# Base products in one fp32r pass, the bias's low part moved to VectorE, embedding norm on VectorE with its constants on ScalarE's queue

## The chip, the core and the metric

The kernel runs on one core of a Trainium2 chip. The engines are PE (TensorE), DVE (VectorE), ACT (ScalarE), POOL (GpSimd) and SP (SyncE, which only issues transfers); each works through its own instruction list in order and waits on semaphores. The metric is the device time of one execution in microseconds. TensorE's clock has two levels here, 1.2 and 2.4 GHz; the profile gives the granted clock as a share of the full one.

## What is computed

The reference chains two transformer blocks over 512 tokens of width 1024. Only the first is touched:

```python
h = _layernorm(jnp.concatenate([meta, x], axis=1), ln_emb_g, ln_emb_b)      # 16 + 512 rows
mix = _mixer(h, ...)                                                         # MLA and GQA attention
h = _layernorm(DEEPNORM_ALPHA * h + mix, ln1_g[i], ln1_b[i])
logits = h @ w_router + b_router;  top_val, top_idx = top_k(logits, 4);  gates = softmax(top_val)
hgu = ragged_dot(h[tok], w_gate_up, group_sizes) + b_gate_up[e_sorted]       # 32 experts
out = ragged_dot(_clamped_swiglu(hgu), w_down, group_sizes) + b_down[e_sorted]
h = _layernorm(DEEPNORM_ALPHA * h + segment_sum(out * gate), ln2_g[i], ln2_b[i])
```

All arithmetic is fp32. Large products are made of fp32r parts: each operand is split into a high part (rounded to fp32r) and a low part (the rest), and the product is high x high + high x low + low x high, each a single-pass matmul. A plain fp32 product is the two-pass matmul that the trace shows as two records.

## The kernel before

Tokens lie in NT = 4 tiles of 128 rows, plus a fifth tile of the 16 meta rows. Every engine's list is written out by hand; `past(name, n)` waits for the n-th signal of that name, `signal` and `put` give one. Buffers are slices of two large SBUF tensors, `act` and `ring`; a name such as `act_parts` in the profile is the same memory seen as fp32r.

**Start.** SP issues the four x tiles, the meta rows, then `colc` (constants in columns, with the epsilon that ACT's square root needs), `lnG`, `lnB` (gain and shift, broadcast to 128 rows), `cm` (the matrices that PE's transposes need) and the weights `w_in` (L1059 to L1071). On DVE, `stats` (L1575, L1578) of tile t runs ahead of `normalise` (L1580 to L1590) of tile t-1: reciprocal, subtract and scale, times gain. POOL's `shift` (L2191 to L2198) adds `lnB`. PE turns each tile (L373), ACT and DVE copy the halves out (L1213, L1622), and block 1's first products follow. The other norms use `affine` on DVE: two `scalar_tensor_tensor` with a reciprocal between them (L1592 to L1606).

**Routing.** After the mixer's output products, `routed_tile` picks four experts a token; then DVE computes gates, ranks and the lists (L1797 to L1900). PE multiplies the one-hot tiles of each token tile into `list_psum`, and DVE takes from it the token list `tl_i`, the places `to_i` and `slot_gate`. POOL then copies a column of the list and gathers 128 rows of `h1_d` (L2277, L2280). Item i of the expert loop is 128 such rows of one expert. Behind the lists DVE splits chunks 4 and 5 of expert 0 (`chunk_low`, L1743); 0 to 3 were split earlier, between the tiles of norm 1.

The bias of gate_up is applied as a 64-row product: `bias2` holds its high part in rows 0 to 31, its low part in rows 32 to 63, and `sel` picks the expert. SP loads `b_gate_up` twice (L1126, L1127) after six chunks of expert 0 and after the last tile of norm 1. POOL adds 1 to the up half (L2264), ACT rounds (L1341), and POOL subtracts to get the low part (L2266). PE waits for `bias_lo` before turning the first rows.

**Item 0.** `turn_rows` (L644), ACT's high part (L1349), DVE's low part `rows_low` (L1912), then `gate_up(0)`: the first half (hh = 0, chunks 0 to 3), `base()`, the second half. `base()` makes the gate-weighted sum of `b_down` for all 512 tokens: 8 products (4 tiles, 2 halves) of `GT` (gates turned to 32 rows by L635, copied by ACT L1343) with `bd` (32 rows) in fp32. DVE adds each to the residual (`base`, L1919), then POOL writes the running sums `acc_d` (L2322, L2323):

```python
for n in range(2 * NT):
    t, hf = n // 2, n % 2
    if n >= 4:
        eng.wait_ge(*past("based", n - 3))
    mm(PS[:, 4 + n % 4, :], GT[:, t, :], bd[:, hf * 512:(hf + 1) * 512]).then_inc(...)
```

SP loads chunks 10 and 11 of expert 0 and chunks 4 to 7 of expert 1 only after the sums' transfers (`sums_begun`, L1130 on).

**Loop.** Each pass loads 12 chunks of 1 MB, ACT rounds them (L1314), DVE makes the low parts (L1743), PE computes gate_up of item i and down of item i-1. PSUM has eight banks: gate_up uses 0 to 3, down 4 and 5, turned rows 6 and 7.

## Time and profile before

| | us |
|---|---|
| median of 3 runs | 2459.7 (2457.81 to 2460.18) |
| the profiled execution | 2455.43, span 2453.6 |
| PE busy | 2321.6 (95%) |
| DVE busy | 1674.0 (68%) |
| ACT busy | 1206.9 (49%) |
| POOL busy | 369.6 (15%) |
| mean DMA rate over the span | 226 GB/s |

"Busy" sums the instructions of an engine; a line can be that of a helper (L365 is `mm`, L373 `turn`'s transpose), so one line holds many products. A bracket behind a row of the timeline says how long the engine had been idle before it and what released it. The windows give, for each stretch, the busy time of each engine (with its count of instructions), the granted clock and the share and rate of the DMA engines.

### The profile page before, as it was taken

How to read it: one execution, taken by the hardware profiler on the slowest of the kernel's cores; microseconds unless marked ns; L12 is line 12 of the kernel's file. 1: busy time of each engine (PE TensorE's matmuls, PEld its weight loads, DVE VectorE, ACT ScalarE, POOL GpSimd, SP SyncE). 2: the span in 40 equal slices, each digit the busy share in tenths (PEclk: the TensorE clock that was granted, in tenths of full speed). 3: DMA queues.
4: the chain of work that ended last, by engine and by line, in shares of the span. 5: the costliest groups of instructions: out<-in, count | busy, mean ns of one | idle time of the engine just before them, and what ended most of it. 6: DMA issues, size and time to landing. Idle time of an engine off the chain costs nothing.

```text
span 2453.6 us, 29282 instructions
## 1 busy us (share of the span) xinstructions
PE 2321.6 (95%) x10464; PEld 1831.5 (75%) x10464; DVE 1674.0 (68%) x1669; ACT 1206.9 (49%) x1189; POOL 369.6 (15%) x267
## 2 busy tenths in 40 slices
PE   5989886999999999999999999959999999999998
PEld 3649654788888888888888888848676787888887
DVE  4535565889889889889988988953555636532434
ACT  1123421767767767776776776723333532331320
POOL 2033002112212212221221221210120001000000
PEclk9999986999999999999999999979999999999999
DMA  8010134999999999999999999772210132322220
GB/s 295 1 52 22 59 143 150 343 384 368 368 392 367 367 388 372 368 383 376 367 378 381 368 374 385 255 265 82 86 48 35 69 122 101 120 77 96 103 103 35
DMA packets 142131, 555.00 MB, mean 226 GB/s; under 512 B 11392, under 2 KB 12416, under 8 KB 125104
## 3 DMA queue, kind: packets, MB, share of 16 engines
q1 hardware_dynamic: 129248, 509.77, 54.6%
q0 software_dynamic: 11088, 40.11, 6.3%
q10 hardware_dynamic: 1728, 4.20, 0.4%
q8 instruction: 45, 0.74, 0.1%
q14 instruction: 22, 0.18, 0.0%
HBM read 525.73 MB, written 28.31 MB: 226 GB/s over the span
## 4 chain that ended last, share of the span: by engine, by line
PE 78%; DVE 3%; ACT 1%; DMA 1%; issue 1%; POOL 0%; DVEq 0%; ACTq 0%; POOLq 0%
PE PS L365 75%; PE PS L650 1%; PE PS L644 1%; ACT ring_parts L1417 0%; DVE ring_parts L1981 0%; DVE act L1601 0%; PE PS L840 0%; DVE st L1575 0%; DVE act L1606 0%; PE PS L750 0%; DMA act<-c_bias_ext 0%; DMA acc_d<-act,to_c 0%; DMA act<-h_d,tl_c 0%; ACT act L1488 0%; DVE act L2178 0%
## 5 line engine op out<-in xcount | busy, mean ns | idle before, releaser
L365 PE MATMUL PS<-act_parts 128*128 128x512 f32 (+2 forms) x3316 | 1064.9, 398 | 23.0 <-DVE act_parts L1891 13.2
L1743 DVE TENSOR_TENSOR low<-ring,act_parts 128x2048 fp32r<-128x2048 f32 x396 | 886.5, 2292 | 45.3 <-ACT act_parts L1314 45.2
L365 PEld LDWEIGHTS PS<-act_parts 128*128 128x128 f32 (+1 forms) x3316 | 622.4, 190 | 189.0 <-issue 58.4
L1314 ACT ACTIVATE act_parts<-ring 128x2048 fp32r<-128x2048 f32 x396 | 732.2, 1911 | 19.1 <-PE PS L365 18.8
L365 PE MATMUL PS<-low,act_parts 128*128 128x512 f32 x1584 | 620.3, 392 | 0.0
L365 PE MATMUL PS<-act_parts,ring_parts 128*128 128x512 f32 (+1 forms) x1280 | 380.1, 388 | 0.6 <-DVE act_parts L2112 0.6
L365 PEld LDWEIGHTS PS<-low,act_parts 128*128 128x128 f32 x1584 | 299.7, 189 | 58.4
L365 PEld LDWEIGHTS PS<-act_parts,ring_parts 128*128 128x128 f32 x1280 | 239.7, 191 | 59.6 <-issue 12.0
L1981 DVE TENSOR_TENSOR ring_parts<-ring,ring_parts 128x4096 fp32r<-128x4096 f32 x30 | 132.7, 4423 | 211.4 <-ACT ring_parts L1417 211.4
L365 PE MATMUL PS<-ring_parts,act_parts 128*128 128x512 f32 x1088 | 262.8, 394 | 2.1 <-DVE act_parts L2144 2.1
L365 PEld LDWEIGHTS PS<-ring_parts,act_parts 128*128 128x128 f32 x1088 | 204.9, 189 | 48.2 <-issue 4.8
L365 PE MATMUL PS<-ring_parts 128*128 128x512 f32 (+1 forms) x608 | 232.3, 382 | 0.0
L365 PE MATMUL PS<-act 128*128 128x128 f32 (+8 forms) x960 | 176.1, 340 | 12.9 <-POOL act L2227 9.6
L1417 ACT ACTIVATE ring_parts<-ring 128x4096 fp32r<-128x4096 f32 x30 | 108.7, 3624 | 136.3 <-PE PS L365 127.9
L365 PEld LDWEIGHTS PS<-act 128*128 128x128 f32 (+2 forms) x960 | 129.7, 196 | 32.9 <-issue 21.4
L1359 ACT ACTIVATE act<-PS 128x512 f32<-128x512 f32 x66 | 39.4, 597 | 206.0 <-PE PS L365 206.0
L365 PEld LDWEIGHTS PS<-ring_parts 128*128 128x128 f32 x608 | 116.2, 191 | 22.2 <-issue 1.5
L2301 POOL DMA_INDIRECT acc_d<-act,to_c x33 | 111.2, 3371 | 27.1 <-POOL to_c L2298 27.1
L1364 ACT ACTIVATE act_parts<-PS 128x512 fp32r<-128x512 f32 x66 | 39.0, 591 | 135.0 <-PE PS L650 135.0
L2287 POOL CAST act_parts<-act 64x128 fp32r (+1 forms) x34 | 59.4, 1748 | 259.2 <-PE PS L365 259.2
L2298 POOL COPY to_c<-to_i 128x1 int32 x33 | 35.2, 1067 | 409.7 <-ACT act L1370 409.7
L365 PE MATMUL PS<-act,ring 128*128 128x512 f32 (+3 forms) x272 | 91.4, 494 | 0.4 <-issue 0.4
(230 smaller groups left out, 1727.5 us busy)
## 6 DMA issues: line engine op xcount, KB each, us to landing
ring<-w_gate_up SPq DMA_DIRECT2D x264, 1024.0 KB, 8.1
ring<-w_down SPq DMA_DIRECT2D x132, 1024.0 KB, 7.5
ring<-w_ff SPq DMA_DIRECT2D x16, 2048.0 KB, 7.7
ring<-w_in SPq DMA_DIRECT2D x12, 2048.0 KB, 9.1
ring<-w_o SPq DMA_DIRECT2D x1, 4096.0 KB, 22.8
ring<-w_out SPq DMA_DIRECT2D x2, 2048.0 KB, 8.4
acc_d<-ring POOLq DMA_DIRECT2D x5, 512.0 KB, 3.1
act<-x SPq DMA_DIRECT2D x4, 512.0 KB, 4.9
```

The source lines that it names most:

```text
L365: return eng.matmul(o, lhsT, rhs, start=first, stop=last, **kw)
L644: ins = eng.transpose(PS[:, 6 + k // 4, k % 4 * P:(k % 4 + 1) * P], xg.rearrange("s (p k) -> s k p", k=KD)[:, k, :], ident)
L650: ins = eng.transpose(PS[:, 6 + hh, j * P:(j + 1) * P], gb[:, hh, :].rearrange("s (m j) -> s j m", j=4)[:, j, :], ident)
L1314: A_(W1hi[c % CS], W1[c], ACT.Copy).then_inc(sem["high"], 1)
L1359: A_(sg[:, hh, :].rearrange("s (b m) -> s b m", b=2), gate_up[:, :, :, 0], ACT.Sigmoid, scale=1.702).then_inc(sem[f"sig_done{hh}"], 1)
L1364: A_(aThi[:, hh, :], PS[:, 6 + hh, :], ACT.Copy).then_inc(sem[f"aT_high{hh}"], 1)
L1417: A_(W2hi[n % NH], W2[n % NW], ACT.Copy).then_inc(signal("w_high"), 1)
L1743: tt(W1lo[c], W1[c], W1hi[c % CS].bitcast(F32), ALU.subtract).then_inc(sem["low"], 1)
L1981: tt(W2lo[n % NW], W2[n % NW], W2hi[n % NH].bitcast(F32), ALU.subtract).then_inc(signal("w_low"), 1)
L2287: eng.tensor_copy(sel, selall[:, bass.ds(n, 1)].to_broadcast([2 * E, P])).then_inc(sem["sel_ready"], 1)
L2298: eng.tensor_copy(to_c[:, :], to_i[:, bass.ds(i - 2, 1)]).then_inc(sem["places_named"], 1)
L2301: eng.indirect_dma_start(out=acc_d, out_offset=bass.IndirectOffsetOnAxis(ap=to_c[:, 0:1], axis=0), in_=yb, in_offset=None, compute_op=ALU. ...
```

## The change

Three parts.

1. Base products: `Gf3` holds, for each tile, the gates' high part, low part and high part again (96 columns); PE turns them to 96 rows `GT`, and `bd3` holds `b_down`'s high part twice and its low part (`bd` is loaded three times; ACT rounds it after `list_psum`, DVE subtracts in rows 64 to 95). One fp32r matmul over 96 rows makes each product. Products 0 to 3 stand ahead of `gate_up`'s first half and use banks 4, 5, 2, 3; products 4 to 7 stand between the halves and use 4 to 7. The second half waits for the first four sums. On DVE the first four sums stand ahead of `chunk_low` of chunks 4 to 7; chunks 4 and 5 are no longer split behind the lists.
2. Bias: SP loads `b_gate_up` after the second tile of norm 1 and ahead of the six chunks; the low part is made by DVE behind the lists. PE waits for `bias_lo` in `gate_up`.
3. Embedding norm: `affine` on DVE in place of `normalise` and POOL's `shift`; `affine` takes 16 rows for the meta tile. ACT issues `colc`, `lnG`, `lnB` and `cm` as its first instructions.

The diff, with most of the unchanged lines left out:

```diff
@@ -85,7 +85,7 @@
...
     "ln_std": [("ln0_std", 5)] + [(f"ln{n}_std", 4) for n in range(1, 5)],
-    "ln_scaled": [("ln0_scaled", 5)],
+    "ln_scaled": [],
     "ln_out": [("ln0_out", 5)] + [(f"ln{n}_out", 4) for n in (1, 2, 3)] + [("ln4_out", 8)],
@@ -219,7 +219,7 @@
...
         Mm = v(R0 + 1248, NT, E)
-        Gf = v(5744, NT, E)
+        Gf = v(R0, NT, E)
         ge = v(R0 + 1504, NT, E)
@@ -242,9 +242,11 @@
...
         OHL = [part(3072, TOPK, 3 * (ITEMS + 1)), part(5120, TOPK, 3 * (ITEMS + 1))]
-        GT = v(5120, NT, P, parts=E)
+        GT = part(5120, NT, P, parts=3 * E)
+        Gf3 = part(5744, NT, 3 * E)
+        bd3 = part(3072, D, parts=3 * E)
         pad = v(5696, ITEMS + 1)
-        bd = v(4096, D, parts=E)
+        bd = v(4096, D, parts=3 * E)
         wr = v(11488, KD, E)
@@ -559,7 +561,7 @@
...
             def router(t):
-                eng.wait_ge(*past("router_in", 48))
+                eng.wait_ge(*past("router_in", 80))
                 eng.wait_ge(*past("h1T_act", t + 1))
@@ -627,12 +629,12 @@
...
 
-            eng.wait_ge(*past("gated", 1))
+            eng.wait_ge(*past("gates_split", 3))
             b = next_bank()
...
             for t in range(NT):
-                ins = eng.transpose(PS[0:E, b, t * P:(t + 1) * P], Gf[:, t, :], ident)
+                ins = eng.transpose(PS[0:3 * E, b, t * P:(t + 1) * P], Gf3[:, t, :].bitcast(F32), ident)
             ins.then_inc(put("gT_psum", b), 1)
@@ -652,7 +654,6 @@
...
             eng.sem_inc(sem["down_used"], 4)
-            eng.wait_ge(*past("bias_lo", 1))
             eng.wait_ge(sem["rows_in"], 16)
@@ -667,18 +668,27 @@
...
 
-            def base():
-                for n in range(2 * NT):
-                    t, hf = n // 2, n % 2
-                    if n >= 4:
-                        eng.wait_ge(*past("based", n - 3))
-                    mm(PS[:, 4 + n % 4, :], GT[:, t, :], bd[:, hf * 512:(hf + 1) * 512]).then_inc(
-                        put("base_psum", 4 + n % 4), 1)
+            def base(n):
+                t, hf = n // 2, n % 2
+                if n == 0:
+                    eng.wait_ge(*past("gT_out", 1))
+                    eng.wait_ge(*past("bd_low", 1))
+                if n >= 4:
+                    eng.wait_ge(*past("based", n - 3))
+                b = (4, 5, 2, 3, 4, 5, 6, 7)[n]
+                mm(PS[:, b, :], GT[:, t, :], bd3[:, hf * 512:(hf + 1) * 512]).then_inc(put("base_psum", b), 1)
 
             def gate_up(i, again=True):
+                if not again:
+                    for n in range(4):
+                        base(n)
                 eng.wait_ge(sem["xT_low"], i + 1)
                 eng.wait_ge(sem["sel_ready"], i + 1)
+                if not again:
+                    eng.wait_ge(*past("bias_lo", 1))
                 for hh in range(2):
+                    if not again and hh:
+                        eng.wait_ge(*past("based", 4))
                     if again:
@@ -692,7 +702,8 @@
...
                     if not again and hh == 0:
-                        base()
+                        for n in range(4, 2 * NT):
+                            base(n)
                 eng.wait_ge(sem["rows_in"], 16 * i + 32)
@@ -1059,12 +1070,6 @@
...
             eng.dma_start(HN[0:META, 4, :], A["meta_tokens"]).then_inc(signal("x4_in", 16), 16)
-            eng.dma_start(colc[:, :], A["c_cols"]).then_inc(signal("cols_in", 16), 16)
-            eng.dma_start(lnG, A["ln_emb_g"].rearrange("(o d) -> o d", o=1).to_broadcast([P, D])).then_inc(
-                signal("ln0_gb", 16), 16)
-            eng.dma_start(lnB, A["ln_emb_b"].rearrange("(o d) -> o d", o=1).to_broadcast([P, D])).then_inc(
-                signal("ln0_gb", 16), 16)
-            eng.dma_start(cm[:, :, :], A["c_mats"]).then_inc(signal("mats_in", 16), 16)
             w_in_v = A["w_in"][0].rearrange("(k p) c -> p k c", p=P)
@@ -1104,7 +1109,8 @@
...
             eng.dma_start(br, A["b_router"].to_broadcast([P, E])).then_inc(signal("router_in", 16), 16)
-            eng.dma_start(bd, A["b_down"][0]).then_inc(signal("router_in", 16), 16)
+            for m in range(3):
+                eng.dma_start(bd[m * E:(m + 1) * E, :], A["b_down"][0]).then_inc(signal("router_in", 16), 16)
 
@@ -1119,12 +1125,12 @@
...
 
+            eng.wait_ge(*past("ln1_out", 2))
+            for half in range(2):
+                eng.dma_start(bgu[half * E:(half + 1) * E, :], A["b_gate_up"][0]).then_inc(signal("bias_in", 16), 16)
             eng.wait_ge(*past("mix_psum", 8))
...
                 load_chunk(0, c)
-            eng.wait_ge(*past("ln1_out", NT))
-            for half in range(2):
-                eng.dma_start(bgu[half * E:(half + 1) * E, :], A["b_gate_up"][0]).then_inc(signal("bias_in", 16), 16)
             for c in range(8):
@@ -1205,6 +1211,12 @@
...
 
+            eng.dma_start(colc[:, :], A["c_cols"]).then_inc(signal("cols_in", 16), 16)
+            eng.dma_start(lnG, A["ln_emb_g"].rearrange("(o d) -> o d", o=1).to_broadcast([P, D])).then_inc(
+                signal("ln0_gb", 16), 16)
+            eng.dma_start(lnB, A["ln_emb_b"].rearrange("(o d) -> o d", o=1).to_broadcast([P, D])).then_inc(
+                signal("ln0_gb", 16), 16)
+            eng.dma_start(cm[:, :, :], A["c_mats"]).then_inc(signal("mats_in", 16), 16)
             eng.wait_ge(*past("cols_in", 16))
@@ -1339,8 +1351,11 @@
...
             A_(bias2, bgu, ACT.Copy).then_inc(signal("bias_hi"), 1)
+            eng.wait_ge(*past("router_in", 80))
+            eng.wait_ge(*past("list_psum", NT))
+            A_(bd3, bd, ACT.Copy).then_inc(signal("bd_high"), 1)
             eng.wait_ge(*past("gT_psum", 1))
-            A_(GT.rearrange("p a b -> p (a b)"), bank_of("gT_psum", 1)[0:E, :], ACT.Copy).then_inc(
+            A_(GT.rearrange("p a b -> p (a b)"), bank_of("gT_psum", 1)[0:3 * E, :], ACT.Copy).then_inc(
                 signal("gT_out"), 1)
@@ -1591,19 +1606,20 @@
...
 
-                parts_ = [X[:, t, m * D // pieces:(m + 1) * D // pieces] for m in range(pieces)]
-                ends = [(X if to is None else to)[:, t, m * D // pieces:(m + 1) * D // pieces] for m in range(pieces)]
-                gains = [G[:, m * D // pieces:(m + 1) * D // pieces] for m in range(pieces)]
-                shifts = [B[:, m * D // pieces:(m + 1) * D // pieces] for m in range(pieces)]
+                n = P if t < NT else META
+                parts_ = [X[0:n, t, m * D // pieces:(m + 1) * D // pieces] for m in range(pieces)]
+                ends = [(X if to is None else to)[0:n, t, m * D // pieces:(m + 1) * D // pieces] for m in range(pieces)]
+                gains = [G[0:n, m * D // pieces:(m + 1) * D // pieces] for m in range(pieces)]
+                shifts = [B[0:n, m * D // pieces:(m + 1) * D // pieces] for m in range(pieces)]
                 eng.wait_ge(*past(f"ln{n_ln}_gb", 32))
...
                 for x, g in zip(parts_, gains):
-                    stt(x, x, mv[:, t, 0:1], g, ALU.subtract, ALU.mult).then_inc(signal("dve_step"), 1)
+                    stt(x, x, mv[0:n, t, 0:1], g, ALU.subtract, ALU.mult).then_inc(signal("dve_step"), 1)
                 eng.wait_ge(*past(f"ln{n_ln}_std", t + 1))
-                eng.reciprocal(rst[:, t:t + 1], std[:, t:t + 1]).then_inc(signal("dve_step"), 1)
+                eng.reciprocal(rst[0:n, t:t + 1], std[0:n, t:t + 1]).then_inc(signal("dve_step"), 1)
                 eng.wait_ge(*latest("dve_step"))
                 for o, x, b in zip(ends, parts_, shifts):
-                    stt(o, x, rst[:, t:t + 1], b, ALU.mult, ALU.add).then_inc(signal(f"ln{n_ln}_out"), 1)
+                    stt(o, x, rst[0:n, t:t + 1], b, ALU.mult, ALU.add).then_inc(signal(f"ln{n_ln}_out"), 1)
 
@@ -1614,8 +1630,8 @@
...
                 if t:
-                    normalise(HN, lnG, 0, t - 1)
-            normalise(HN, lnG, 0, 4)
+                    affine(HN, lnG, lnB, 0, t - 1)
+            affine(HN, lnG, lnB, 0, 4)
             for t in range(5):
@@ -1755,7 +1771,7 @@
...
                 chosen = slice(TOPK * t, TOPK * (t + 1))
-                eng.wait_ge(*past("router_in", 48))
+                eng.wait_ge(*past("router_in", 80))
                 eng.wait_ge(*past("iotas_in", 1))
@@ -1898,8 +1914,16 @@
...
             tt(slot_gate, slot_gate, listed[:, 2 * I1:3 * I1], ALU.add).then_inc(signal("gates_listed"), 1)
-            for c in range(4, CS):
-                chunk_low(0, c)
+            eng.wait_ge(*past("bias_hi", 1))
+            tt(bias2[E:2 * E, :], bgu[E:2 * E, :], bias2[E:2 * E, :].bitcast(F32), ALU.subtract).then_inc(
+                signal("bias_lo"), 1)
+            eng.tensor_copy(Gf3[:, :, 0:E], Gf).then_inc(signal("gates_split"), 1)
+            eng.tensor_copy(Gf3[:, :, 2 * E:], Gf).then_inc(signal("gates_split"), 1)
+            eng.wait_ge(*latest("gates_split"))
+            tt(Gf3[:, :, E:2 * E], Gf, Gf3[:, :, 0:E].bitcast(F32), ALU.subtract).then_inc(signal("gates_split"), 1)
+            eng.wait_ge(*past("bd_high", 1))
+            tt(bd3[2 * E:3 * E, :], bd[2 * E:3 * E, :], bd3[2 * E:3 * E, :].bitcast(F32), ALU.subtract).then_inc(
+                signal("bd_low"), 1)
             eng.wait_ge(*past("lam_exp", 1))
@@ -1955,10 +1979,12 @@
...
 
-            for c in range(CS, 8):
+            for n in range(4):
+                base(n)
+            for c in range(4, 8):
                 chunk_low(0, c)
             swiglu(0, 0, again=False)
-            for n in range(2 * NT):
+            for n in range(4, 2 * NT):
                 base(n)
@@ -2199,7 +2225,6 @@
...
                 eng.memset(rows, 0.0).then_inc(signal("zero_rows"), 1)
-            shift(HN, lnB, 0, 5)
 
@@ -2262,11 +2287,7 @@
...
             ts(up, up, 1.0, None, ALU.add).then_inc(signal("bias_one"), 1)
-            eng.wait_ge(*past("bias_hi", 1))
-            tt(bias2[E:2 * E, :], bgu[E:2 * E, :], bias2[E:2 * E, :].bitcast(F32), ALU.subtract).then_inc(
-                signal("bias_lo"), 1)
-            eng.wait_ge(*past("bias_lo", 1))
-
+            eng.wait_ge(*latest("bias_one"))
             eng.wait_ge(*past("tokens_listed", 1))
```

## Rows read from the trace of the kernel before

**Rows 1.** Chain of waits from 385.5 us on: start us, length us, what.

```profile
385.53 5.98 DMA act<-h_d,tl_c
...
396.03 37.59 PE PS L365 x116
...
478.26 23.57 PE PS L365 x100
...
514.60 23.56 PE PS L365 x100
```

**Rows 2.** Windows: stretch, length, busy us of each engine, clock, DMA share, GB/s.

```profile
0.00:7.50 7.50, 0.00 (x0) 0.00 (x0) 2.92 (x7) 1.28 (x1) 3.19 (x8) 1.00 0.76 280
...
396.00:409.80 13.80, 13.77 (x50) 10.59 (x50) 4.58 (x2) 5.12 (x3) 0.00 (x0) 0.84 0.62 207
415.00:416.70 1.70, 1.70 (x3) 0.66 (x2) 1.00 (x2) 0.00 (x0) 0.54 (x1) 0.50 0.82 325
437.00:439.00 2.00, 1.36 (x8) 1.32 (x8) 2.00 (x2) 2.00 (x2) 0.00 (x0) 0.77 1.03 424
475.00:1565.00 1090.00, 1090.00 (x4919) 883.86 (x4918) 991.35 (x630) 782.17 (x540) 239.92 (x150) 1.00 1.01 375
```

**Rows 3.** Timeline of the start: start us, busy us, engine, line, operation, [idle before <-releaser].

```profile
4.54 1.29 DVE L1575 BATCH_NORM_STATS2 st<-act 128x6 f32<-128x512 f32 x2 [3.69 <-DMA act<-x]
...
12.18 1.22 DVE L1590 TENSOR_TENSOR act<-act 128x1024 f32<-128x1024 f32 x1 [1.60 <-DMA act<-ln_emb_b]
...
13.56 2.34 POOL L2198 TENSOR_TENSOR act<-act 128x1024 f32<-128x1024 f32 x1 [9.85 <-DVE act L1590]
...
30.30 2.47 DVE L1622 COPY act<-PS 128x512 f32<-128x512 f32 x4
...
34.23 41.08 PE L365 MATMUL PS<-act,ring 128*128 128x512 f32 x120 [0.36 <-issue]
```

**Rows 4.** Timeline of VectorE at the norm of block 1's third tile.

```profile
331.18 0.69 DVE L1782 SCALAR_TENSOR_TENSOR act<-act,PS 128x512 f32<-128x512 f32 x1 [4.14 <-PE PS L365]
331.90 1.29 DVE L1575 BATCH_NORM_STATS2 st<-act 128x6 f32<-128x512 f32 x2
...
334.94 1.29 DVE L1606 SCALAR_TENSOR_TENSOR ring<-act,rst 128x1024 f32<-128x1024 f32 x1
```

**Rows 5.** Timeline of the lists, VectorE and GpSimd.

```profile
371.67 2.94 POOL L2264 TENSOR_SCALAR act<-act 64x1024 f32<-64x1024 f32 x1 [84.90 <-DMA act<-b_gate_up]
371.77 1.58 DVE L1881 TENSOR_TENSOR act_parts<-act 128x512 fp32r<-128x512 f32 x1
...
373.27 0.35 DVE L1883 TENSOR_TENSOR act_parts<-act 128x192 fp32r<-128x192 f32 x1
...
376.51 0.68 DVE L1881 TENSOR_TENSOR act_parts<-act 128x512 fp32r<-128x512 f32 x1
376.63 4.93 POOL L2266 TENSOR_TENSOR act_parts<-act,act_parts 32x2048 fp32r<-32x2048 f32 x1 [2.02 <-ACT act_parts L1341]
...
377.12 4.66 DVE L1883 TENSOR_TENSOR act_parts<-act 128x192 fp32r<-128x192 f32 x1
```

**Rows 6.** Timeline between the lists and item 0.

```profile
384.97 4.48 DVE L1743 TENSOR_TENSOR low<-ring,act_parts 128x2048 fp32r<-128x2048 f32 x2
385.53 2.68 POOL L2280 DMA_INDIRECT act<-h_d,tl_c  x1 [0.89 <-DVE to_i L1897]
...
394.72 1.00 POOL L2280 DMA_INDIRECT act<-h_d,tl_c  x1 [0.79 <-POOL tl_c L2277]
...
396.03 1.94 PE L365 MATMUL PS<-act_parts 64*128 64x512 f32 x3 [2.44 <-DVE act_parts L1912]
```

**Rows 7.** Timeline of item 0 around the base products.

```profile
409.83 9.75 PE L365 MATMUL PS<-act 32*128 32x512 f32 x16
...
419.51 1.94 PE L365 MATMUL PS<-act_parts 64*128 64x512 f32 x3
419.69 0.69 DVE L1919 SCALAR_TENSOR_TENSOR ring<-ring,PS 128x512 f32<-128x512 f32 x1 [1.02 <-PE PS L365]
```

## The prediction

> **What bounds the kernel now.** I read the chain of waits first. From 385.5 us on it names one engine nearly alone: PE, whose pieces repeat with each pass of the expert loop, every 36.34 us (a run of 100 matmuls at 478.26, the next at 514.60, and so on to 1556), and PE has no idle time in these passes [rows 1, 2]. The queue of loads is as full as PE there (DMA share 1.01 at 375 GB/s), but PE's matmuls follow each other without a gap, so PE sets the pace. The change touches no instruction of that loop. It touches three places ahead of it, and what it wins or loses there is worth its full length, because nothing later waits for a fixed time. The three, read next in the timeline: the embedding norm up to the first product of block 1 (0 to 34.2 us); the routing and its lists, where DVE works nearly without a break and PE waits (353 to 384); item 0 (396 to 439). The windows give the granted clock of these stretches [rows 2].
>
> **Start: constants by ScalarE's queue, the norm on VectorE.** Before, SP issues four x tiles, the meta rows, then colc, gain and shift, all in one queue. DVE stands 1.60 us until shift is in, at about 12.1 [rows 3]. Then each tile costs DVE 4.2 us, POOL adds the shift in 2.34 us, PE turns, and so on; the first product starts at 34.23 [rows 3]. DVE's copies of the turned halves (2.47 us) start at 30.30, beside POOL's last shift, and cost nothing.
> After: constants and x are issued side by side from about 0.7 us. If the two queues share the engines evenly, shift lands when twice its own queue's 1.06 MB have moved. The first 7.5 us move 280 GB/s, 2.1 MB [rows 2]. I add 0.8 us, an estimate, from the last byte to its use: 8.3 us. The second x tile, on the other queue, also lands at about 8.3. From there DVE is alone on the path: statistics 1.5 us, then the affine form of two 1.29 us instructions and a reciprocal, 2.7 us as ln1's rows show (statistics from 331.90, the second of the two ends at 336.23), so 4.25 a tile [rows 4]. 8.3 + 1.5 + 2.7 = 12.5 for tile 0; three more pairs, 25.2; the meta tile, 27.9 (16 rows take the time of 128); now the copies are no longer covered, since POOL's last shift is gone: 2.7 us, 30.6; product at about 31.0. **Gain 3.2 us.** Bounds: if gain and shift still land at 12.1, the affine starts there and the product at 33.3 (0.9 us); if they never hold DVE up and x keeps its pace, DVE's whole work of 5 x 4.25 + 2.7 runs from 4.54 [rows 3] to 28.5, product at 28.8, gain 5.4. w_in comes behind the same bytes as now, and no product waits for it today. ScalarE only waits in this stretch; its four issues cost no one anything.
> The Trainium skill, page "DMA: Bandwidth & Descriptors", section "Queues, rings and completion order", says that each DMA engine takes turns between the queues with work, a packet at a time. No row here has two queues loading at the start, so the trace doesn't test it. Were it wrong and x first, as now, the constants would land as late as now and the start would give its lower bound; were the constants first, x would be what is late.
>
> **Router: bias low part and its loads.** The bias loads stand behind 6 MB of expert chunks in SP's queue; POOL waits 84.9 us for them, so that its +1 starts at 371.67 and its subtraction at 376.63, in the middle of the lists [rows 5]. Beside them two DVE instructions stretch: an L1881 takes 1.58 instead of 0.68 us, an L1883 4.66 instead of 0.35, ending with POOL's 4.93 us instruction [rows 5]. DVE has no idle time from there to L1891, and the last list product waits for it. The change issues the bias loads at ln1_out 2 (about 320) into an idle queue, so POOL's +1 runs at about 323; the subtraction goes to DVE behind gates_listed. Both stretches vanish: 0.90 + 4.31 = **5.2 us**. At 323 POOL can hold DVE's second chunk_low up for its 2.94 us; DVE idles 4.14 us before the residual sum at 331.18, which covers it, and without that cover it would cost the 2.9 [rows 4, 5]. bd is loaded three times instead of once (256 KB more) near 292 with the DMA queues idle: nothing.
> New work behind the lists: on DVE the subtraction (32 x 2048), two casts and a subtraction of Gf3, and bd_low (32 x 1024). By 2.24 us for 128x2048, 1.22 for 128x1024 and three small ones of 0.2 [rows 3, 6]: 4.2 us, in place of two chunk_low, 4.48 us, which move behind the base sums. On ACT one more copy (96 x 1024, about 1.1 us). Counted with the times of before, less 5.2: lists end at 379.9, gates_split at 382.9, transposes (1.05 us) at 384, gT_out at 384.7, bd_low at 384.2; the rows of gather 0 land at 386.3. So PE still waits for the gather, with 1.6 us to spare. Bounds: if the subtraction takes POOL's 4.93 us on DVE too, gT_out is at 387.3 and 1.0 us of the gain is lost. The first gather takes 2.68 us on POOL beside two-input DVE work and lands after 5.98, the second 1.00 [rows 1, 6]: the new DVE work stands at the same place, I take 5.98 again; 1.7 us less is possible.
> The Trainium skill, "SBUF — State Buffer", section "Who interferes with whom", says that an SBUF-to-SBUF copy on VectorE in a two-port mode locks GpSimd out of writing DMA descriptors. That speaks against the two new Gf3 casts, which run beside this gather; no row here shows the pair.
>
> **Item 0: base products.** Now 16 matmuls (8 products in two fp32 passes each) on 32 rows take PE from 409.83 to 419.51, 9.68 us [rows 7], with the chain and expert work standing still. They run slowly at the end, where the granted clock has fallen to 0.50 (1.2 GHz) inside them, and the second half of gate_up starts in that clock: 14.1 us to 433.62, where a half at full clock takes 23.57 / 2 = 11.8 [rows 1, 2, 7]. After: products 0 to 3 go ahead of gate_up, in PE's gap of 2.4 us between turning rows (to 393.6) and the first product (396.03) [rows 6]. One fp32r matmul of 512 columns takes 0.236 us at full clock (23.57 / 100) and so 0.47 at half: 1.9 us, hidden, and its four sums on DVE (0.69 each) start when rows_low is done. Products 4 to 7 stand between the halves: banks 4 to 7 and all sums they wait for are free by then; four at 0.236 us, 0.9, with a little for the start, 1.0. Terms: 9.68 - 1.0 = **8.7 us**; second half at full clock, 14.1 - 11.8 = **2.3 us**; first half now 13.8 (to 409.83) at a mean clock of 0.84 [rows 2]: PE is busy 2 us longer before it, so the rise may come up to 2.0 us (its whole loss) earlier, or not at all; I take **0.9**. chunk_low 4 to 7 now follow the base sums: 2.8 + 4 x 2.24 puts chunk 4 at 5.0 us and chunk 7 at 11.8 after the start of gate_up; PE wants them at 12.7 and about 22: covered. SP's next loads wait for the sums' transfers. The last sum on DVE now ends 24.4 us after the start of item 0 [rows 7]; after, it follows the first half (12.9), ACT's sigmoid, three 0.7 us steps and four sums at about 18.4, so loads start 6 us earlier, but PE is 11.9 us shorter: they stand 5.9 us nearer to PE. Six chunks of 1.05 MB at 375 GB/s take 17 us; the last, chunk 7 of item 1, lands some 10 us after item 1 starts, and PE wants it after 22: no price.
>
> **Sum.** 3.2 + 5.2 + 8.7 + 2.3 + 0.9 = 20.3 us. The profiled execution took 2455.4 (span 2453.6), 4.3 under the runs' median of 2459.7. Profile: 2435.1; runs: 2459.7 - 20.3 = **2439.4 us**.
>
> **Rivals.** (a) Constants don't come sooner (contention with x): start gives 0.9, total 18.0, 2441.7. For it: after the first 7.5 us with 2.1 MB, the 1.05 MB of gain and shift took 4.6 us more, 228 GB/s, so their bytes may be slow ones [rows 2, 3]. Chance 0.2. (b) The gather's issue is held up: it takes 2.68 us beside DVE work and 1.00 alone [rows 6]; were POOL held for all 4.2 us of the new DVE work rather than the 1.7 it loses now, the gather lands 2.5 us later. Total 17.8, 2441.9. Against: what differs in kind from now are the casts, 0.2 us each. Chance 0.1. (The Trainium skill's section on who interferes with whom, named above, has the lock that would do it.) (c) The clock doesn't behave: the 96-row products don't keep it up, the second half stays at 14.1 and the first at 13.8. For it: it fell inside the present base products. Total 17.1, 2442.6. Against: these are 0.9 us, not 9.7. Chance 0.1. (d) Slower: the expert loop. Its DMA share is 1.01, and item 1 begins with 5.9 us less lead of the loads. If the loads became what the loop runs at, each of some 32 passes would lengthen; from 0.63 us a pass (1.7%, 20.3 us in all) the gain is gone; at 1 us a pass, 2459.7 + 11.7 = 2471.4. Against: an item moves 36.35 x 375 = 13.6 MB, at the 424 GB/s of 437 to 439 us 32.1 us, so 4.2 us of each pass are spare and the lead is back in two passes [rows 2]. Chance 0.05. (e) The change's waits line up worse than drawn (bias_one at 323, bd_high behind list_psum, the sums of the base before chunk_low), so that only a part of the router's and item 0's terms comes: about 10 us, 2449.7. Chance 0.1.
>
> **How the numbers follow.** Forecast 0.45, (a) 0.2, (b) 0.1, (c) 0.1, (e) 0.1, (d) 0.05. The low end adds the upper bounds: 5.4 + 5.2 + 1.7 + 8.9 + 2.3 + 2.0 = 25.5, 2434, and 2 us for the spread of the runs, 2432. The high end adds the lower ones, 0.9 + 4.2 + 8.5 + 0 + 0 = 13.6, 2446, and 2 us: 2448. (e) and (d) are left out. About 0.2%, 4.9 us, is what a measurement of this kernel can tell from no change. Slower by more than that only in (d), 0.04; within it, 0.04, parts of (d) and (e); faster 0.92.
>
> **What would show it.** Right: first L365 product at about 31; no L1883 above 0.4 us; last list product near 374.6 (382.9 - 5.2 - 3.2); base matmuls 8, four between rows and gate_up; clock 1.00 through the second half, which takes 11.8 us; item 1 starting some 20 us sooner, and 36.35 a pass as before. Wrong: a first affine later than 9.8; POOL's gather issue above 2.7 us; PE waiting for DVE in item 0 or for low chunks in item 1; a pass of the loop longer than 36.4.

## The result and the profile after

| | before | after |
|---|---|---|
| median, us | 2457.81 (2455.45 to 2460.18, 5 runs) | 2431.51 (2430.19 to 2431.99, 5 runs) |
| ratio | | 0.9892 [0.9878, 0.9905] |
| profiled execution, span | 2455.43, 2453.6 | 2431.09, 2429.2 |

The gain is 26.3 us by the medians and 24.4 by the spans of the two profiled executions; 20.3 was forecast. 2431.51 lies half a microsecond below the range of 2432 to 2448. A later execution of the kernel before took 3390.06 us at a mean granted clock of 0.65, against 0.97 in the others, and stands in no median here.

The chain of waits of after (start us, length us, what) answers [rows 1]:

```profile
376.37 6.09 DMA act<-h_d,tl_c
...
382.50 1.99 PE PS L646 x8
...
386.92 24.56 PE PS L367 x104
...
417.61 24.30 PE PS L367 x98
...
454.69 23.57 PE PS L367 x100
...
491.03 9.06 PE PS L367 x38
```

The gather starts 9.16 us sooner than in [rows 1]; item 0's piece takes 24.56 in place of 37.59; item 1's run starts at 417.61 here because its first two products, from 416.63, are a piece of their own; in before it was one piece of 100, which took 26.15 from 439.32 on. The run at 454.69 is the one that stood at 478.26: 23.57 us are won there, and it has the same length. Nothing moves in the loop: the same lead is found at its end (1606.64 in before, 1583.07 in after). The last 0.8 us of the gain by spans come after it, most of them (0.6) right behind the last item, where a `to_c` instruction of POOL on the path takes 1.94 us in place of 3.27; why is open.

Windows of after (stretch, length, busy us of each engine, clock, DMA share, GB/s) answer [rows 2]:

```profile
384.00:386.00 2.00, 2.00 (x7) 1.27 (x5) 0.36 (x1) 1.02 (x1) 0.57 (x2) 0.50 0.00 0
386.00:388.00 2.00, 1.26 (x5) 0.67 (x5) 2.00 (x4) 0.00 (x0) 0.61 (x1) 0.91 0.27 72
...
400.00:412.00 12.00, 12.00 (x57) 9.82 (x56) 3.79 (x7) 0.50 (x1) 1.88 (x4) 1.00 0.84 306
...
418.00:420.00 2.00, 2.00 (x6) 1.52 (x6) 2.00 (x2) 2.00 (x2) 0.00 (x0) 0.50 0.99 391
...
440.00:1540.00 1100.00, 1100.00 (x4968) 892.34 (x4967) 1003.46 (x639) 787.91 (x545) 242.96 (x152) 1.00 1.01 376
```

The clock is back at its upper level (2.4 GHz) from about 386.4 and stays there to the end of item 0; it is at the lower one again as item 1 begins, behind a wait of PE for the turned rows. The last line is the loop, as full as before.

Timeline of after at the start, answering [rows 3]:

```profile
7.72 1.28 DVE L1590 BATCH_NORM_STATS2 st<-act 128x6 f32<-128x512 f32 x2 [1.76 <-DMA act<-x]
...
10.76 1.28 DVE L1617 SCALAR_TENSOR_TENSOR act<-act,mv 128x1024 f32<-128x1024 f32 x1 [1.52 <-DMA act<-ln_emb_b]
...
13.36 1.28 DVE L1590 BATCH_NORM_STATS2 st<-act 128x6 f32<-128x512 f32 x2
...
17.34 1.28 DVE L1590 BATCH_NORM_STATS2 st<-act 128x6 f32<-128x512 f32 x2
...
30.58 5.75 PE L367 MATMUL PS<-act,ring 128*128 128x512 f32 x8 [1.36 <-issue]
```

The first affine waits for the shift until 10.76, 2.5 us later than drawn; the first product starts at 30.58 in place of 34.23.

Timeline of after at the lists and the gather, answering [rows 5] and [rows 6] (the first two lines are the +1 on the bias and what DVE did beside it):

```profile
317.46 4.48 DVE L1759 TENSOR_TENSOR low<-ring,act_parts 128x2048 fp32r<-128x2048 f32 x2
320.58 4.14 POOL L2289 TENSOR_SCALAR act<-act 64x1024 f32<-64x1024 f32 x1 [37.69 <-DMA act<-b_gate_up]
...
372.26 0.35 DVE L1899 TENSOR_TENSOR act_parts<-act 128x192 fp32r<-128x192 f32 x1
...
375.92 2.28 DVE L1918 TENSOR_TENSOR act_parts<-act,act_parts 32x2048 fp32r<-32x2048 f32 x1
...
376.37 2.80 POOL L2301 DMA_INDIRECT act<-h_d,tl_c  x1 [0.88 <-DVE to_i L1913]
378.23 0.23 DVE L1920 CAST act_parts<-act 128x128 fp32r<-128x128 f32 x1
...
382.50 1.97 PE L646 MATMUL PS<-cm,act 128*128 128x128 f32 x8 [2.44 <-DMA act<-h_d,tl_c]
384.13 2.05 PE L367 MATMUL PS<-act_parts 96*128 96x512 f32 x4
```

All four L1899 and L1897 take 0.35 and 0.68 us; the 4.66 and the 1.58 of [rows 5] are gone. The first four base products lie in PE's gap. PE still waits 2.44 us for the gather.

### The profile page after: what moved, and what is told of

The parts are those of the page before. It is cut to its first block, busy times and chain, and to the rows that moved or that the text cites. A ratio compares the mean times of both kernels' runs of the same rounds, so it can differ in the third digit from the quotient of the medians.

```text
span 2429.2 us, 29268 instructions
## 1 busy us (share of the span) xinstructions
PE 2309.9 (95%) x10456; PEld 1826.7 (75%) x10456; DVE 1670.6 (69%) x1674; ACT 1208.5 (50%) x1190; POOL 355.2 (15%) x261
## 4 chain that ended last, share of the span: by engine, by line
PE 79%; DVE 3%; ACT 1%; DMA 1%; issue 1%; POOL 0%; DVEq 0%; ACTq 0%; POOLq 0%
PE PS L367 75%; PE PS L652 1%; PE PS L646 1%; ACT ring_parts L1432 0%; DVE ring_parts L2007 0%; DVE act L1617 0%; PE PS L851 0%; DVE st L1590 0%; DVE act L1622 0%; PE PS L761 0%; DMA act<-c_bias_ext 0%; DMA acc_d<-act,to_c 0%; DMA act<-h_d,tl_c 0%; ACT act L1503 0%; DVE low L1759 0%
## 5 line engine op out<-in xcount | busy, mean ns | idle before, releaser
L367 PE MATMUL PS<-act 128*128 128x128 f32 (+7 forms) x944 | 166.9, 334 | 12.8 <-POOL act L2252 9.6
L367 PEld LDWEIGHTS PS<-act 128*128 128x128 f32 (+1 forms) x944 | 126.6, 197 | 27.9 <-issue 17.7
```

The costliest lines, as they stand in the source:

```text
L367: return eng.matmul(o, lhsT, rhs, start=first, stop=last, **kw)
```

## Experiments

Ratios are to runs of the kernel before on the same chip. Over all of them that kernel has 48 runs, median 2456.6. The quoted texts say what was expected before each run.

**One part alone.** Each starts from the kernel before and takes one of the three parts whole, as in the diff above: p_start (`affine`, four loads on ScalarE's queue), p_bias (loads after `ln1_out` 2, subtraction on DVE in place of POOL's), p_base (96 rows, places of the products and sums; POOL keeps the bias subtraction).

> The kernel before with the start alone: affine norm on VectorE, four constant loads on ScalarE's queue. Theory 'the parts add up': the profile of after has the first block 1 product at 30.6 instead of 34.2 us, so 3.6 us less. Rival 'the parts help each other': clearly less than 3.6 alone, and the rest of the 24 to 26 us comes only with the others. If it is faster by 5 or more, something behind 34 us gains too.

> The kernel before with the bias part alone: loads after norm 1's second tile, low part by VectorE behind the lists. Theory: 5.2 us less, the two stretched VectorE instructions of the lists being the whole of it. Rival: the extra 2.3 us of VectorE work beside the first gather takes part of it back: 3 to 4 us.

> The kernel before with the base products alone (96 rows, one fp32r pass, four ahead of gate_up), bias low part still on GpSimd, start as before. Theory of the prediction: 11.9 us less. Rival 'clock': PE enters the first half of gate_up and item 1 at the full clock or closer to it, 14 to 15 us less, with 11.7 us instead of 13.8 for the first half and item 1's 26.15 us run of matmuls shortened by more than 1 us.

| | median, us | ratio | against the 2456.71 beside them | by spans | term(s) |
|---|---|---|---|---|---|
| p_start | 2451.79 (11 runs) | 0.9982 [0.9973, 0.9991] | -4.9 | -4.4 | 3.2 |
| p_bias | 2449.64 (10 runs) | 0.9974 [0.9965, 0.9984] | -7.1 | -6.7 | 5.2 |
| p_base | 2441.55 (5 runs) | 0.9934 [0.9921, 0.9948] | -15.2 | -13.9 | 11.9 |

The three sum to 27.2 us by medians and 25.0 by spans. Together they bring 25.2 against the same 2456.71 and 24.4 by spans, so the parts add up to within 2 us, which is also what two executions of one kernel differ by (below). Each brings 1.2 to 3.3 us more than its term. In p_base item 1 wins nothing (from its turned rows to the end of its run 27.84 us, in before 27.85), so the rival 'clock' holds for the first half alone. p_base leaves the bias on POOL, and there the stretched instruction is still in the lists. Timeline of p_base:

```profile
377.31 4.92 POOL L2289 TENSOR_TENSOR act_parts<-act,act_parts 32x2048 fp32r<-32x2048 f32 x1 [2.03 <-ACT act_parts L1353]
...
377.80 4.65 DVE L1899 TENSOR_TENSOR act_parts<-act 128x192 fp32r<-128x192 f32 x1
```

Item 0 of p_base takes 24.56 us as in after. Its runs stand apart, two at 2438.2 and 2438.7 and three at 2441.6 to 2442.4, and the profile is of one of the slower ones: a fast item 0 doesn't alone make a fast execution.

**The constants back on SP's queue** (a_consts_sp, and a_consts_sp2 once more), with `affine` kept:

```diff
             eng.dma_start(HN[0:META, 4, :], A["meta_tokens"]).then_inc(signal("x4_in", 16), 16)
+            eng.dma_start(colc[:, :], A["c_cols"]) ...
+            eng.dma_start(lnG, ...); eng.dma_start(lnB, ...); eng.dma_start(cm[:, :, :], A["c_mats"]) ...
```

> The changed kernel with the four constant loads back on SyncE's queue behind x: tells the queue from the move of the norm. Theory of the prediction: constants land at 12.1 as before, first product at 33.3 us, 2.3 to 2.7 us slower than the changed kernel (30.6). Rival: constants behind x gain nothing because x then lands sooner, within 1 us of the changed kernel.

Timeline of a_consts_sp, VectorE at the start:

```profile
12.28 1.28 DVE L1617 SCALAR_TENSOR_TENSOR act<-act,mv 128x1024 f32<-128x1024 f32 x1 [4.92 <-DMA act<-ln_emb_b]
```

DVE stands 4.92 us, until the shift is in at 12.28, and the first product is at 32.10, where 33.3 was expected. So of the start's 3.65 us, 1.52 (32.10 - 30.58) are the second queue's and 2.13 (34.23 - 32.10) the norm's form. The median, 2437.46 (ratio 0.9924 [0.991, 0.9937]), is 5.95 above after's, too much for 1.5 us at the start: four of its five runs lie at 2437.0 to 2439.1 and one, the profiled one, at 2431.64. That split is followed up below.

> The constants on SyncE's queue once more: its five runs lay at 2431.6 and four times 2437 to 2439, and the profile was that of the lowest. A profile of the slower case should show where 6 us go. Theory: PE's half clock, in block 1's first products (which start after a longer wait) or in block 2. Rival: a transfer that lands late at the start, 3 us or more at the first product.

It gave 2438.22; the first product is at 32.34 and item 0 takes 27.54 us, where the profiled execution of a_consts_sp had 24.56.

**Form and place of the base products.** a_base_between leaves them in one fp32r pass over 96 rows, but puts all eight between the halves, with their sums behind `swiglu`; a_fp32_split leaves the places and takes the 32-row fp32 form back.

```diff
 # a_base_between
-                if not again:
-                    for n in range(4):
-                        base(n)
...
                     if not again and hh == 0:
-                        for n in range(4, 2 * NT):
+                        for n in range(2 * NT):
                             base(n)
 # a_fp32_split
-                mm(PS[:, b, :], GT[:, t, :], bd3[:, hf * 512:(hf + 1) * 512]) ...
+                mm(PS[:, b, :], GT[:, t, :], bd[0:E, hf * 512:(hf + 1) * 512]) ...
```

> The changed kernel with all eight fp32r base products between the halves of gate_up, as in the kernel before; only their form stays new. Tells form from place. Theory 'the gap that they fill is worth something by itself': PE stands 2.4 us ahead of item 0 and the first half runs at half clock again for some 4 us (13.8 us, against 11.7 in the changed kernel), and the eight products wait for VectorE's sums, about 5 us on PE instead of 1: 6 to 7 us slower than the changed kernel. Rival 'form is all': at most 2 us slower.

> The changed kernel with the old form of the products (32 rows, fp32, two matmuls each) in the new places. Theory: place alone can't carry it. Four products at half clock take 4 x 1.7 us where the gap has 2.4, so gate_up starts about 4.4 us later, and the four between the halves take 3.4 instead of 0.9: 7 us slower than the changed kernel. By the clock rival the first half is then at half clock as well: 2 us more.

a_base_between: 2442.54 (2441.82 to 2444.4), ratio 0.9948 [0.9934, 0.9961]. a_fp32_split: 2446.0 (2443.89 to 2449.73), ratio 0.996 [0.9946, 0.9974]. They lie 11.0 and 14.5 us above after, where 6 to 7 and 7 to 9 were expected: the first halves and the products cost about what was drawn, the second halves were drawn at full clock and didn't run at it. Chain of waits of a_base_between:

```profile
387.70 14.80 PE PS L367 x50
...
407.61 15.39 PE PS L367 x51
```

Between the halves pass 5.1 us (402.5 to 407.6), in after 1.0: products 4 to 7 wait for sums that DVE, busy with low parts and `swiglu`, makes late. Then the second half begins at the lower clock again (0.50 over 408 to 414) and takes 15.4 in place of 11.8. Timeline of a_fp32_split, PE:

```profile
384.19 7.19 PE L367 MATMUL PS<-act 32*128 32x512 f32 x8
...
405.32 3.69 PE L367 MATMUL PS<-act 32*128 32x512 f32 x8
```

The first four products in the old form take 7.19 us at the lower clock, where the gap has room for some 2.5: gate_up starts 9.0 us after the first turned rows (391.31 - 382.29), in after 4.4. The other four take 3.69 (1.0 in after), and behind them the windows show 0.50 again, from about 410 to 413. From the first turned row to the end of item 0: before 41.98 us, new form in the old place 39.7, old form in the new place 40.1, both new 28.98 (32.01 in a_again, below). Either alone brings about 2 us, both 13 or 10. The products have to be short to fit the gap, and the sums have to be early so that nothing waits. With either one missing the clock falls between the halves and the second half pays: behind a wait of PE in a_base_between, behind the 32-row products in a_fp32_split.

**The gather ahead of the new DVE work.** In g_gather_first DVE makes the small gate parts, waits for `sel_ready` (which POOL gives behind the gather's issue), and only then does the two large subtractions.

```diff
-            tt(bias2[E:2 * E, :], bgu[...], bias2[...], ALU.subtract).then_inc(signal("bias_lo"), 1)
             eng.tensor_copy(Gf3[:, :, 0:E], Gf) ...
+            eng.wait_ge(sem["sel_ready"], 1)
             eng.wait_ge(*past("bd_high", 1))
             tt(bd3[2 * E:3 * E, :], ...).then_inc(signal("bd_low"), 1)
+            tt(bias2[E:2 * E, :], bgu[...], bias2[...], ALU.subtract).then_inc(signal("bias_lo"), 1)
```

> The changed kernel with VectorE's two large subtractions behind the lists (32 x 2048 and 32 x 1024) waiting for GpSimd's selector copy, which stands behind the issue of the first gather; the small gate copies go first. Theory 'VectorE's two-input work delays the gather's issue': issue 1.0 instead of 2.8 us, landing after 4.3 to 4.5 instead of 6.1, whole kernel 1.7 us faster than the changed one. Rival: the first gather is slow for a reason of its own (first use), no change.

Timeline of g_gather_first, POOL, and then its chain of waits:

```profile
375.64 1.09 POOL L2302 DMA_INDIRECT act<-h_d,tl_c  x1 [0.88 <-DVE to_i L1913]
```

```profile
375.64 4.67 DMA act<-h_d,tl_c
...
380.36 1.98 PE PS L646 x8
...
384.77 26.44 PE PS L367 x104
...
416.49 26.59 PE PS L367 x100
```

The issue takes 1.09 in place of 2.80 us and the rows land after 4.67 in place of 6.09; they are turned 2.1 us earlier than in after (0.7 of it from ahead of the gather). Yet the median is 2432.89 (2430.74 to 2434.72, ratio 0.9905 [0.9889, 0.992]): the clock is at 0.50 until 388 and at 1.00 only from 390, so item 0 takes 1.9 us more, and item 1, from its turned rows to the end of its run, 1.4 us more (27.84 in place of 26.40). What the transfer gives, the clock takes, and more: the loop starts 1.2 us later than in after (455.86 against 454.69). The 1.7 us that were expected of the whole kernel did not come.

> The kernel before once more, for a second profile. Theory 'executions differ by where the clock's rises fall': its span differs from the first profile's 2453.6 by up to 3 us, and the difference lies in the length of half-clock stretches (the first half of gate_up, the first matmuls of item 1, the router). Rival: the difference lies in the loop or in block 2.

The kernel before, profiled again: item 1's run 26.16 (26.15 the first time), the gather 0.65 us sooner, and yet a span 2.6 us longer. In the second block a run of 48 matmuls takes 14.02 us in place of 12.51 and one of 93 takes 22.91 in place of 21.39; the windows show 0.50 over 1952 to 1956 in b_again, and 0.60 and then 1.00 in the first profile. So some 2.5 us of difference between two executions need no cause in the change.

**Two groups of runs.** After was run again, and with spare matmuls into an unused bank, in w_route ahead of norm 1's last turned tile, in w_all at four gaps of PE (ahead of that tile, on both sides of the gates' transposes, ahead of item 1) on top of g_gather_first:

```diff
+            def warm(b, n):
+                for _ in range(n):
+                    mm(PS[:, b, :], ident, cm[:, 0:4, :].rearrange("p a b -> p (a b)"))
...
+            warm(cur[0] % 8, 3)
             turn_tile(NT - 1)
```

> The changed kernel once more, beside the others on the same chip, with a second profile. Theory: 2431.5 again. Item 0 from turned rows to item 1's first matmuls differs between its profiles by the clock alone: if the rise falls late, the first half of gate_up takes about 13.8 instead of 11.7 us, so that the 13.0 us that the first profile shows for item 0 are the lucky case.

> The changed kernel with three idle matmuls (identity times constants, 128 x 512 fp32, result overwritten) in the 2.8 us for which PE waits for the last tile of norm 1. Theory 'half clock after a gap costs what the text of the profile shows': the last turn 1.04 instead of 1.94 us, the last router product 1.87 instead of 3.59, the ranks about 1 instead of 1.92, all on the path: 3 to 3.5 us faster than the changed kernel. Rival: the three matmuls don't hold the clock, or delay the turn: no change or slower.

> As w_route, with the gather issued ahead of VectorE's large subtractions (g_gather_first), and idle matmuls also ahead of turning the gates, ahead of turning the first rows and in the gap between items 0 and 1. In g_gather_first the gather came 2.1 us sooner and the half clock of item 0 and 1 took it back. Theory 'that was the clock': with PE busy in the gaps, item 0 starts 2 us sooner and at full clock, item 1's 100 matmuls take 23.6 instead of 24.3 to 26.5: 6 to 8 us faster than the changed kernel. Rival: the idle matmuls stand in the way, under 3 us.

| | runs, us | item 0 in the profile | ratio |
|---|---|---|---|
| a_again | 2431.45, 2436.25, 2436.78, 2436.82 | 27.60 | 0.9908 [0.9891, 0.9925] |
| w_route | 2433.99 to 2435.61 (4) | 27.78 | 0.9908 [0.9892, 0.9925] |
| w_all | 2427.57 to 2429.16 (4) | 24.55 | 0.988 [0.9864, 0.9897] |

Chain of waits of a_again (2436.82 us), the same kernel as after:

```profile
377.99 6.24 DMA act<-h_d,tl_c
...
384.28 1.99 PE PS L646 x8
...
388.69 27.60 PE PS L367 x104
...
422.27 25.24 PE PS L367 x100
...
460.30 23.57 PE PS L367 x100
```

and its windows:

```profile
392.00:394.00 2.00, 2.00 (x6) 1.52 (x6) 2.00 (x2) 0.00 (x0) 0.00 (x0) 0.50 0.95 379
394.00:400.00 6.00, 6.00 (x25) 4.85 (x24) 3.72 (x2) 3.69 (x2) 0.00 (x0) 0.89 0.55 181
```

Of the 5.6 us by which its loop starts later than after's (460.30 against 454.69), 3.04 are item 0. A stretch of 6 us with mean clock 0.89 between the levels 0.50 and 1.00 has 1.3 us at the lower one, so the clock rises at 395.3, 11.0 us after the first turned rows; by the same working after's rise is at 386.4, 3.9 us after them. The last 0.8 are in item 1.

1.8 us are lost before the rows are turned. 0.17 of them is the start of block 1's first product, and 0.94 comes until ScalarE copies its bank out (40.98 against 39.87). PE's weight loads (PEld) in that product, in after and then in a_again:

```profile
34.13 0.34 PEld L367 LDWEIGHTS PS<-act,ring 128*128 128x128 f32 x1 [0.52 <-issue]
34.89 0.19 PEld L367 LDWEIGHTS PS<-act,ring 128*128 128x128 f32 x1 [0.42 <-issue]
35.32 0.19 PEld L367 LDWEIGHTS PS<-act,ring 128*128 128x128 f32 x1 [0.24 <-issue]
```

```profile
36.00 0.34 PEld L367 LDWEIGHTS PS<-act,ring 128*128 128x128 f32 x1 [0.52 <-issue]
36.85 0.20 PEld L367 LDWEIGHTS PS<-act,ring 128*128 128x128 f32 x1 [0.52 <-issue]
37.29 0.19 PEld L367 LDWEIGHTS PS<-act,ring 128*128 128x128 f32 x1 [0.24 <-issue]
```

They stand 0.85 us apart up to 34.13 in after and up to 36.85 in a_again, and 0.43 behind that. So PE kept half pace for about two loads more (0.43 us each), although the windows show 1.00 over the whole of it; I take it for the lower clock, since the pace is just half, and conclude that the column of the windows doesn't show it this early in the execution. Another 0.5 goes at 165 to 172, where the windows of 168 to 172 show 1.00 in after and 0.75 in a_again, and 0.2 ahead of and in the gather. a_third has the same losses (0.5, 0.96 and 0.5 at these three places).

w_route does part of what was expected of it ahead of the lists: the last turn takes 1.09 us in place of 1.97, the router's product 2.72 in place of 3.60, and the gather starts at 375.12, 1.25 us sooner than in after. But it does not get the early rise, and item 0 loses 3.2 us, so the 3 to 3.5 us did not come. w_all, which is busier in the gaps next to the gather, has both item 0 (24.55) and item 1 at the upper clock, and gains 3.3 us on after where 6 to 8 were expected.

Whether that was its doing or luck was the last question. w_gather is after with four of the spare matmuls only, two on each side of the gates' transposes:

```diff
             b = next_bank()
             eng.wait_ge(*free[b])
+            warm(b, 2)
             eng.wait_ge(*past("gates_split", 3))
...
+            warm(0, 2)
```

> The full change plus four spare matmuls on PE in the stretch where it waits for the lists and the gather: two ahead of the gates' transposes, two behind them, all before the first rows are turned. Theory M (what PE does just before it turns the first rows decides how soon the clock rises): the clock rises within some 2 us of the turning, in the profile item 0's 104 matmuls take 24.5 to 24.6 us, and all timed runs lie near 2431 with none near 2436.5. Theory N (the rise is drawn anew in each execution, whatever PE does in the gap): the runs fall into the two groups of the full change, 2430 to 2432 and 2436 to 2437, in a like share; item 0 takes 24.6 or 27.6.

> The full change a third time. So far six of nine runs lie at 2430.2 to 2432.0 and three at 2436.3 to 2436.8, and the two profiles, one of each group, differ in item 0 (24.56 against 27.60 us). Expected of both theories: again both groups, nothing between 2432.5 and 2435.5, and a profile whose item 0 is 24.6 in the first group and 27.6 in the second.

> The full change with the gather ahead of VectorE's large subtractions and spare matmuls at four gaps, again. It took 2427.6 to 2429.2 in four runs. Theory M: again all runs within 2 us of 2428, 3 below the full change's faster group (the gather lands earlier) and 8.5 below its slower one. Theory N: some runs near 2433.

Windows of w_gather:

```profile
382.00:384.00 2.00, 1.81 (x5) 0.88 (x6) 0.00 (x0) 0.00 (x0) 0.00 (x0) 1.00 0.36 141
...
388.00:390.00 2.00, 2.00 (x5) 1.40 (x5) 2.00 (x5) 0.00 (x0) 0.60 (x1) 0.50 0.73 242
...
392.00:394.00 2.00, 2.00 (x11) 1.65 (x10) 2.00 (x2) 1.20 (x1) 0.00 (x0) 1.00 0.61 188
```

In this profile the rise comes at 381, ahead of the turned rows at 384.15; but PE is busy only 0.52 us of 386 to 388, while ACT and DVE split the rows, and the clock falls once more until about 391. Item 0 takes 26.11, and the runs, 2431.08, 2431.64, 2433.89 and 2435.51 (ratio 0.9904 [0.9887, 0.992]), are two in the first group and two between the groups. Both theories fail as put. Work ahead goes with an earlier rise: in w_gather, w_all and w_all2 it lies ahead of the turned rows, and in no profile without spare matmuls beside the gather does it. But in w_gather the early rise isn't kept through the next gap.

a_third gave 2430.39, 2430.57, 2430.78 and 2436.92 (ratio 0.9897 [0.9881, 0.9914]), and the profile of the last has item 0 at 27.61. Over its 13 runs after has nine at 2430.2 to 2432.0, four at 2436.2 to 2436.9 and none between. w_all2 gave 2428.11, 2428.20, 2430.51 and 2434.62 (ratio 0.9896 [0.988, 0.9913]), so the theory that all its runs lie within 2 us of 2428 fails too. Chain of waits of w_all2 (the execution of 2430.51):

```profile
382.76 0.89 PE PS L654 x8
...
386.08 24.57 PE PS L367 x104
...
416.78 23.00 PE PS L367 x98
```

Both items are at the upper clock again, in two profiles of two. w_all and w_all2 are one kernel; over its eight runs the median is 2428.5, three below after's 2431.5 over thirteen, with the spare matmuls and the earlier gather together (no run has all the spare matmuls without the earlier gather); it is the fastest version, though not free of slower runs.

## Why the prediction was wrong

The direction, the places and most mechanisms held; the size was short. Two steps failed: the reference point that the sum was taken off, and terms at PE's clock, of which item 1's was missing and the first half's was a middle value. By the profiled executions the 7.9 us between 2439.4 and 2431.5 are about half the one and half the other.

**The reference point, 3.9 us.** I forecast 2435.1 for the profiled execution and added 4.3, because before's profiled execution lay 4.3 under the median of three runs. After's profiled execution lies 0.4 under its own median. 3.1 of the 3.9 are the median of three, which was high: over 48 runs it is 2456.6. The step that failed is "2459.7 - 20.3": a difference of one profile from a median of three was carried over as if it were a property of the kernel. From 2456.6 the same terms give 2436.3 and a range from 2429 to 2445, which holds the result. There is some luck in the miss, too: after's five runs were all of its faster group, which has nine of 13, and the slower ones, at 2436 to 2437, lie inside the range as it was given.

**The terms, 24.4 in place of 20.3 by the spans.** The 4.1 us are 0.45 at the start, 0.3 in the lists, 1.1 in item 0, 1.4 in item 1 and 0.8 behind the loop.

- Start: 3.65, forecast 3.2. The two steps behind it were both off and nearly cancelled. The shift came at 10.76, not 8.3; a tile costs DVE 3.98 (13.36 to 17.34), not 4.25, which I had added up from pieces that overlap a little when DVE never waits. DVE used the wait for a second tile's statistics, as in before, which I had not counted. Rival (a) is out: 1.5 us are the queue's. Its price of 0.9 for the start was wrong for the same reason: with the constants behind x, a_consts_sp still gains 2.13.
- The two queues, for x and for the constants, do share. The issues of the first 60 us (KB each, median us to landing), of before and of after:

```profile
act<-x SPq DMA_DIRECT2D x4, 512.0 KB, 4.9
act<-ln_emb_b SPq DMA_DIRECT2D x1, 512.0 KB, 8.0
```

```profile
act<-x SPq DMA_DIRECT2D x4, 512.0 KB, 7.7
act<-ln_emb_b ACTq DMA_DIRECT2D x1, 512.0 KB, 9.1
```

  x lands later by 2.8 us and the shift 1.4 us sooner (issued at 1.64, not 4.09). This agrees with what the Trainium skill states in "DMA: Bandwidth & Descriptors", section "Queues, rings and completion order": the engines take turns between queues.
- Lists: 5.5 (9.16 less 3.65), forecast 5.2. As drawn: both stretches gone. The +1 cost POOL 4.14 us beside `chunk_low` and DVE nothing: its two low parts take 4.48 us there as in before, and the idle time that was to cover a loss (4.13 us before the residual sum at 327.27) wasn't needed.
- Behind the lists: 0, forecast 0. The DVE subtraction takes 2.28, as taken from the 128-partition row. Rival (b) named a real cost, already in before: g_gather_first takes 1.7 us off the issue and with it 1.4 off the landing. It was as large in before, where no cast stood near it (2.68 against 2.80), so it moved nothing, and the casts add nothing that shows: p_bias, without them, has 2.80 too. What costs is the DVE subtraction that began ahead of the issue. The issue ends 1.0 us behind that one's end in after (379.17 and 378.20), p_bias (382.36 and 381.38) and before (388.21 and about 387.2). In p_base the two-input 32x1024 subtraction starts at 386.36, behind the issue's start at 386.21, and the issue takes 1.09.
- Base products and second half: 8.7 + 2.3 forecast; four are hidden, four take 1.0 (398.7 to 399.7), the second half 11.8 at full clock. Both right. a_base_between and a_fp32_split show that neither would stand without the other, which the terms, simply added, did not say.
- First half: 0.9 forecast, inside bounds of 0 and 2.0. After's profile has the upper bound, 11.8 us at full clock. But a_again and a_third have 14.8 (3.04 more), a loss of 1.0 that lies outside the bounds. The step failed in kind: it took a middle value for something that came out near one end or beyond the other.
- Item 1: no term, 1.4 won (from its turned rows at 415.50 to the end of its run at 441.90 26.40 us, in before 27.85 from 437.63). It ran at the lower clock for less time. In p_base and g_gather_first the same stretch takes 27.84, so this gain isn't the change's in every execution. I read [rows 2] only as far as item 0; the window at 437 to 439, used for its rate, shows a clock of 0.77 that I passed over. With it (26.15 less 23.57, 2.6 us) the low end would have held the result.
- Rival (d) is out: item 1's first product starts 22.6 us sooner (416.63 against 439.25) and the loop's pass is 36.34 us (454.69 to 491.03) as before, with the same DMA share. Rival (e) is out too. Of rival (c), the clock, a part came: no profile of the changed kernel shows it in the second half. The first half is slow in both profiles from the slower group, and that group is four runs of 13, 5 us above the others with what lies around it.
- Three of the signs named for a wrong forecast did appear: the first affine at 10.76 (later than 9.8), a gather issue of 2.80 us (above 2.7), and PE waiting for a low part in item 1. The first two are priced above, and the third stood in before as well (a weight load idle 0.68 us behind DVE's low part, in before 0.65). None of them says why the forecast was short: they all point at a slower kernel.

## What to carry to other kernels

Take the reference from many runs, or compare spans of profiles with each other; do not add the distance between one profile and a small median. Where a stretch before or after a stall runs at a reduced clock, list every such stretch in the windows down to the loop, price each at both clock levels, and expect that the kernel's time may fall into groups instead of spreading around the middle. Take profiles of both groups before you explain one of them. A short product that is moved into a gap costs nothing there and can help PE's next work; test its form and its place together, since here either alone gave 2 us and both gave 13 or 10.

## What the runs showed of the hardware

- The time from the first turned rows to the full clock isn't fixed. Worked out from the windows, in profiles without spare matmuls, it is 8.7 to 10.9 us in the five with the gap before item 0 empty (before 8.8, b_again 8.9, p_start 8.7, p_bias 10.5, a_base_between 10.9). In the seven with the four fp32r products in the gap it is 3.2 (p_base), 3.5 (a_consts_sp), 3.9 (after), 8.6 (g_gather_first), 10.9 (a_consts_sp2), 11.0 (a_again) and 11.1 (a_third); in w_route, whose spare matmuls lie far ahead of the gap, 11.3. An early rise was seen only with the gap filled, but in three of these eight. A gap in which PE was busy 0.52 of 2 us was followed by a fall to 0.50 in w_gather, and in w_all a gap as short (0.49 of 2 us at 386 to 388) was not. What decides it stays open.
- The clock also fell where the windows show PE busy throughout: inside the 32-row fp32 products in before (1.00 at 413 to 414, 0.50 at 415 to 416), and right behind four of them in a_fp32_split (0.92 at 409 to 410, then 0.50). Around the four 96-row fp32r products between the halves, in after, a_again and a_third, the windows show 1.00. Rows, passes and length changed together, so which of them matters isn't shown.
- An indirect gather's issue on POOL took 2.80 us when a 32x2048 two-input subtraction had begun on DVE 0.45 us ahead of it, and 1.09 when none had (g_gather_first) or when a shorter one began 0.15 us behind it (p_base); the landing took 6.09, 4.67 and 4.43. The Trainium skill, "SBUF — State Buffer", section "Who interferes with whom", says that a VectorE instruction with two inputs in SBUF contends with a GpSimd instruction that reads SBUF. If the gather's issue, which takes its row numbers from `tl_c` in SBUF, counts as such a read, the trace agrees with it. The trace also shows that the issue ends 1.0 us behind the DVE instruction that began first, as if it had waited for that one.
- It goes the other way too: a DVE instruction of 128x192 that began 0.49 us behind POOL's 32x2048 subtraction took 4.65 us in p_base, in place of 0.35, and ended 0.2 behind it. The same shape takes 0.35 in after, where POOL has no such instruction.
- POOL's +1 over 64x1024 took 2.94 us in [rows 5] and 4.14 where DVE's 128x2048 subtraction was already running: 1.36 until that one ended (321.94), and 2.78 more.
- The clock column of the windows shows 1.00 over block 1's first product, while PE's weight loads stand 0.85 us apart at first and 0.43 later. Early in these executions the pace of the rows tells more than the column.
